# Hybrid decoder block on one core: row statistics spread by DMA, the merge moved into the next step, squares in two fp32r parts

## The reference, cut to what matters

```python
q = rmsnorm(qkv[:, :, 0], q_norm_g[i]) * scale
k = rmsnorm(qkv[:, :, 1], k_norm_g[i])
...
for g, (window, dilation) in enumerate(ATTN_PATTERNS):
    o_g, lse_g = dilated_window_attention(q[:, :, g], k[:, :, g], v[:, :, g], slopes[g], window, dilation)
...
# inside: m = max(s); p = exp(s - m); den = sum(p); o = p @ v / den; lse = m + log(den)
wgt = jax.nn.softmax(jnp.stack(lses, axis=0), axis=0)
o_attn = jnp.sum(wgt[..., None] * jnp.stack(outs, axis=0), axis=0)
```

## Time and profile before

| what | us |
|---|---|
| median of 3 runs | 1835.39 |
| lowest and highest | 1834.36, 1835.42 |
| the profiled execution, whole | 1834.99 |
| its span in the profile | 1833.2 |
| TensorE busy in the span | 1788.0 (98%) |
| VectorE, ScalarE, GpSimd busy | 1024.3, 561.8, 828.6 |

### The profile page before, as it was taken

How to read it: one execution, slowest core, us unless ns; L and a number is a source line. 1 busy time by engine, 2 the same in 40 slices (tenths; PEclk the granted TensorE clock), 3 DMA queues, 4 the chain that set the end, 5 groups by cost and what they waited for, 6 DMA issues and landing times.

```text
span 1833.2 us, 23679 instructions
## 1 busy us (share of the span) xinstructions
PE 1788.0 (98%) x8628; PEld 1420.7 (77%) x8628; DVE 1024.3 (56%) x1545; ACT 561.8 (31%) x1069; POOL 828.6 (45%) x597
## 2 busy tenths in 40 slices
PE   8999999999999987999999999999999999999997
PEld 6777777777777766788888888788888888888786
DVE  6346645564655488343313323787787887644644
ACT  6533444354245423111411222533333333000000
POOL 7536443644544374554225734265455455222221
PEclk9999999999999999999999999999999999999999
DMA  4111111211121023445412244322232232345211
GB/s 173 36 41 47 52 53 41 64 52 41 41 58 47 24 70 93 112 114 132 144 64 70 92 141 169 138 82 90 69 93 79 69 103 92 137 150 194 81 54 49
DMA packets 64192, 158.08 MB, mean 86 GB/s; under 512 B 10912, under 2 KB 27680, under 8 KB 64112
## 3 DMA queue, kind: packets, MB, share of 16 engines
q1 hardware_dynamic: 51856, 145.35, 24.5%
q10 hardware_dynamic: 11792, 10.04, 1.9%
q0 software_dynamic: 464, 1.62, 0.2%
HBM read 123.54 MB, written 32.26 MB: 85 GB/s over the span
## 4 chain that ended last, share of the span: by engine, by line
PE 85%; DVE 8%; issue 3%; POOL 2%; DMA 1%; ACT 1%; SPq 0%; DVEq 0%; POOLq 0%
PE bank L911 13%; PE bank L912 13%; PE bank L913 13%; PE bank L1276 7%; PE bank L1278 7%; PE bank L1277 7%; PE bank L1334 4%; PE bank L1336 4%; PE bank L1335 4%; PE bank L925 2%; PE bank L1059 2%; PE bank L1072 2%; PE bank L1045 2%; DVE run_z L1774 1%; PE bank L1238 1%
## 5 line engine op out<-in xcount | busy, mean ns | idle before, releaser
L911 PE MATMUL bank<-hhi,whi 128*128 128x512 f32 x1024 | 421.0, 411 | 5.6 <-DVE hlo L1711 5.6
L912 PE MATMUL bank<-hlo,whi 128*128 128x512 f32 x1024 | 404.9, 395 | 0.0
L913 PE MATMUL bank<-hhi,wlo 128*128 128x512 f32 x1024 | 404.8, 395 | 0.0
L626 POOL TENSOR_TENSOR wlo<-raw,whi 128x1024 fp32r<-128x1024 f32 (+1 forms) x84 | 196.7, 2342 | 300.1 <-DVE whi L1667 298.1
L911 PEld LDWEIGHTS bank<-hhi,whi 128*128 128x128 f32 x1024 | 193.7, 189 | 52.5 <-issue 10.1
L913 PEld LDWEIGHTS bank<-hhi,wlo 128*128 128x128 f32 x1024 | 193.6, 189 | 45.4
L912 PEld LDWEIGHTS bank<-hlo,whi 128*128 128x128 f32 x1024 | 194.1, 190 | 39.5 <-issue 1.2
L1824 DVE CUSTOM_DVE_ANT_0 sp<-bank,mask 128x128 f32<-128x128 f32 (+1 forms) x192 | 56.3, 348 | 114.6 <-PE bank L1045 112.7
L1449 ACT ACTIVATE sp<-sp,negm 128x128 f32<-128x128 f32 (+1 forms) x192 | 83.9, 439 | 106.6 <-DVE negm L1828 106.5
L884 POOL TENSOR_TENSOR plo<-st,phi 128x512 fp32r<-128x512 f32 x60 | 79.5, 1328 | 58.6 <-ACT phi L1579 57.4
L2114 DVE CAST fhi<-ff 128x1024 fp32r (+1 forms) x44 | 31.4, 715 | 125.4 <-PE bank L1336 125.4
(11 more groups left out here) (304 smaller groups left out, 3927.8 us busy)
## 6 DMA issues: line engine op xcount, KB each, us to landing
raw<-in_wblocks SPq DMA_DIRECT2D x98, 512.0 KB, 3.6
pair<-in_wblocks SPq DMA_DIRECT2D x40, 512.0 KB, 4.8
ff_scr<-ffo SPq DMA_DIRECT2D x22, 512.0 KB, 5.9
ff<-ff_scr SPq DMA_DIRECT2D x22, 512.0 KB, 4.2
rt<-rt_scr SPq DMA_DIRECT2D x8, 516.0 KB, 6.6
x<-in_xT SPq DMA_DIRECT2D x8, 512.0 KB, 9.2
zb_scr<-zb SPq DMA_DIRECT2D x8, 512.0 KB, 3.3
zb<-zb_scr SPq DMA_DIRECT2D x8, 512.0 KB, 3.5
```

The lines of the kernel that those rows point to most:

```text
L626: pool.tensor_tensor(wlo[par][:, 0:cols], raw[par][:, 0:cols], whi[par][:, 0:cols].bitcast(F32), ALU.subtract).then_inc(lo_done, 1)
L911: nc.tensor.matmul(ps, a, x, start=start and k == k_list[0], stop=False)
L912: nc.tensor.matmul(ps, a, y, start=False, stop=False)
L913: last = nc.tensor.matmul(ps, b, x, start=False, stop=stop and k == k_list[-1])
```

## The change

- `sum_squares` becomes two fp32r matmuls: ScalarE writes the square twice, rounded (`sqh`) and in fp32 (`sq`); VectorE subtracts (`square_lo`, tile `sql`), between `merge_max` and the merge weights, or between `merge_psum` and `merge_z`. It moves to the end of sub-steps 2, 4, 6, 8.
- In steps 0 to 10 the copies and 16 transposes of the statistics are replaced: one transpose of both statistics (32 rows) at j = 9, a copy to SBUF by ScalarE at j = 10, and `spread` on SP: a store to DRAM, a wait for it, and four loads that write a row into 64 partitions each, into the tile `bmd` (after pattern 0 straight into `run_n` and `run_z`).
- The merge of steps 0 to 10 moves as a whole into the next step: `merge_max` and weights at j = 1 and 5, `merge_psum` and `merge_z` at j = 3 and 7, GpSimd's part at j = 4 and 8, ScalarE's exponential at j = 3 and 7. It reads `bmd` in SBUF in place of PSUM. The product with v at j = 4 and 8 waits for it. Step 11 keeps its own merge at its end and gets that of step 10 before it.

```diff
-        stat = [hx[:], rtmp[:].rearrange("p a g k -> p (a g k)")]
+        negm, den = sd[:, 0], sd[:, 1]
+        stat = [bmd[:, h, :] for h in range(2)]
+        LAST = 3 * HP - 1
...
+            def spread(a, hp, ag):
...
+                sp_.wait_ge(st_copied, a + 1)
+                sp_.wait_ge(d_read, 2 * a + 1)
+                if ag == 0 and hp:
+                    sp_.wait_ge(o_ready, 2 * hp)
...
+                sp_.dma_start(stat_scr.rearrange("i x (s q) -> (i x s) q", q=P), st_t[0:32, :]).then_inc(st_out, 16)
+                sp_.wait_ge(st_out, 16 * (a + 1))
+                for i, done in enumerate((sm_in, sz_in)):
+                    to = (run_n, run_z)[i][:, :] if ag == 0 else bmd[:, i, :]
+                    for x in range(2):
+                        sp_.dma_start(to[DH * x:DH * (x + 1)], stat_scr[i, x].unsqueeze(0).broadcast_to([DH, T])).then_inc(done, 16)
...
             for hp in range(HP - 1):
...
+                for b in range(3):
+                    loop_load(hp, b)
+                if hp:
+                    spread(3 * hp - 1, hp - 1, 2)
+                for b in range(3, 6):
+                    loop_load(hp, b)
+                spread(3 * hp, hp, 0)
+                for b in range(6, 9):
+                    loop_load(hp, b)
+                spread(3 * hp + 1, hp, 1)
+                loop_load(hp, 9)
...
+            spread(LAST - 3, HP - 2, 2)
...
+            spread(LAST - 2, HP - 1, 0)
...
+            spread(LAST - 1, HP - 1, 1)
...
             def rescale(ag, hp, h):
...
+                if ag == 2:
+                    pool.wait_ge(merged, hpc(hp, 2) + 2)
...
-                    if a and ag == 0 and j == 0:
-                        weigh(a - 1, 2, hp - 1, 1)
-                    if a and ag == 0 and j == 5:
-                        normalise(2, hp - 1, 1)
+                    if a and ag != 1 and j in (4, 8):
+                        pg, ph, h = (ag + 2) % 3, hp - (ag == 0), j // 4 - 1
+                        rescale(pg, ph, h)
+                        weigh(a - 1, pg, ph, h)
+                    if a and ag == 0 and j in (7, 10):
+                        normalise(2, hp - 1, j == 10)
+                    if a and ag == 0 and j == 10:
...
-                    if a is not None and ag > 0 and j in (10, 11):
...
+                    if n is None and j in (10, 11):
...
-                        if ag == 1 or n is None or h == 0:
-                            weigh(a, ag, hp, h)
-                        if ag == 2 and n is None:
-                            normalise(ag, hp, h)
-                        elif ag == 2 and h:
-                            normalise(ag, hp, 0)
+                        weigh(a, ag, hp, h)
+                        normalise(ag, hp, h)
...
             def sum_squares(n, gi):
...
-                pe.wait_ge(sq_done, 4 * n + gi + 1)
-                nc.tensor.matmul(b_nb[:], blk_ones, sq[:, gi % 2, :], start=True, stop=True).then_inc(ss_done, 1)
+                pe.wait_ge(sql_done, 4 * n + gi + 1)
+                nc.tensor.matmul(b_nb[:], ones_r[:], sqh[:], start=True, stop=False)
+                nc.tensor.matmul(b_nb[:], ones_r[:], sql[:], start=False, stop=True).then_inc(ss_done, 1)
...
-                    if n is not None and j in (2, 4, 6, 8):
-                        gi = (j - 2) // 2
-                        if gi == 0:
-                            pe.wait_ge(vev_done, 2 * a + 2)
-                        else:
-                            pe.wait_ge(ln_done, 4 * n + gi)
-                        sum_squares(n, gi)
-                    if a is not None and j in (9, 11):
+                    if n is None and j in (9, 11):
...
-                    if a is not None and j in (10, 11):
+                    if n is None and j in (10, 11):
...
+                                if a and s_ % 4 == 0:
+                                    pe.wait_ge(d_read, 2 * a + s_ // 4)
...
+                        if n is not None and j == 9:
+                            pe.wait_ge(ln_done, 4 * n + 4)
+                            nc.tensor.transpose(b_nb[0:32, 0:P], sd[:].rearrange("p i x s -> p (i x s)"), ident).then_inc(mt_done, 1)
+                    if n is not None and j in (2, 4, 6, 8):
+                        gi = (j - 2) // 2
+                        if gi == 0:
+                            pe.wait_ge(vev_done, 2 * a + 2)
+                        else:
+                            pe.wait_ge(ln_done, 4 * n + gi)
+                        sum_squares(n, gi)
...
             def square(n, g, b, gi):
...
-                if gi >= 2:
-                    act.wait_ge(ss_done, 4 * n + gi - 1)
-                act.activation(sq[:, gi % 2, :].rearrange("p (i r) -> p i r", r=DIL[g]),
-                               by_residue((qn if gi < 2 else kn)[g][:, :], g, gi % 2), ACT.Square).then_inc(sq_done, 1)
+                if gi:
+                    act.wait_ge(ss_done, 4 * n + gi)
+                x = by_residue((qn if gi < 2 else kn)[g][:, :], g, gi % 2)
+                act.activation(sqh[:].rearrange("p (i r) -> p i r", r=DIL[g]), x, ACT.Square)
+                act.activation(sq[:, gi % 2, :].rearrange("p (i r) -> p i r", r=DIL[g]), x, ACT.Square).then_inc(sq_done, 1)
...
+            def weights_exp(ag, hp, h):
...
+                act.wait_ge(ab_in, 4 * hp + 2 * (ag - 1) + h + 1)
+                act.activation(ab[h][:], ab[h][:], ACT.Exp).then_inc(ab_exp, 1)
...
             def slot(n, g, b, a, ag, hp):
                 for j in range(12):
+                    if a and ag != 1 and j in (3, 7):
+                        weights_exp((ag + 2) % 3, hp - (ag == 0), j // 4)
...
-                    if a is not None and ag and j >= 10:
-                        h = j - 10
-                        act.wait_ge(ab_in, 4 * hp + 2 * (ag - 1) + h + 1)
-                        act.activation(ab[h][:], ab[h][:], ACT.Exp).then_inc(ab_exp, 1)
-                        if ag == NPAT - 1 and h:
+                    if a is not None and n is not None and j == 10:
+                        act.wait_ge(mt_done, a + 1)
...
+                        act.activation(st_t[0:32, :], b_nb[0:32, 0:P], ACT.Copy).then_inc(st_copied, 1)
+                    if a and ag == 0 and j in (5, 9):
+                        reciprocal_z(hp - 1, NPAT - 1, j == 9)
+                    if n is None and j >= 10:
+                        weights_exp(ag, hp, j - 10)
+                        if j == 11:
...
-                    if a and ag == 0 and j == 3:
-                        reciprocal_z(hp - 1, NPAT - 1, 1)
...
+                if first:
+                    act.wait_ge(merged, 4 * HP + 2)
...
             def ublock(hp, n):
-                a = 3 * hp + 1
-                merge_psum(a, 1, hp, 1)
-                evict_u(hp, n, 0)
-                merge_z(a, 1, hp, 1)
-                evict_u(hp, n, 1)
+                for h in range(2):
+                    evict_u(hp, n, h)
...
             def merge_max(a, ag, hp, h):
-                dve.wait_ge(mt_done, 2 * a + h + 1)
-                nn, ps = natural(run_n[:, :], ag, h), split2(b_nb[:], ag)
                 if ag == 0:
-                    V.tensor_copy(nn, ps).then_inc(m_read, 1)
...
+                if a == LAST:
+                    dve.wait_ge(mt_done, LAST + h + 1)
+                else:
+                    dve.wait_ge(sm_in, 32 * (a + 1))
+                nn, new = natural(run_n[:, :], ag, h), split2(b_nb[:] if a == LAST else half(bmd[:, 0, :], h), ag)
+                up = split2(ab[h][:, 1, :], ag)
...
-                link(TT(up, nn, ps, ALU.subtract))
-                TT(nn, nn, ps, ALU.min).then_inc(m_read, 1)
+                link(TT(up, nn, new, ALU.subtract))
+                link(TT(nn, nn, new, ALU.min))
+                if a == LAST:
+                    dve.sem_inc(m_read, 1)
...
+            def merge_weights(a, ag, hp, h):
+                if ag == 0:
+                    return
+                down, up = (split2(ab[h][:, i, :], ag) for i in range(2))
...
             def merge_psum(a, ag, hp, h):
...
-                dve.wait_ge(dt_done, 2 * a + h + 1)
+                if a == LAST:
+                    dve.wait_ge(dt_done, h + 1)
+                else:
+                    dve.wait_ge(sz_in, 32 * (a + 1))
...
-                    V.tensor_copy(nm, split2(b_o[h][:], ag))
-                    V.tensor_copy(nz, split2(b_t[:], ag)).then_inc(d_read, 1)
+                    V.tensor_copy(natural(num[:, :], ag, h), split2(b_o[h][:], ag)).then_inc(d_read, 1)
...
-                TT(t_z[:], b_t[:], ab[h][:, 1, :], ALU.mult).then_inc(d_read, 1)
+                TT(t_z[:], b_t[:] if a == LAST else half(bmd[:, 1, :], h), ab[h][:, 1, :], ALU.mult).then_inc(d_read, 1)
...
             def merge_z(a, ag, hp, h):
...
+            def square_lo(n, gi):
...
+                dve.wait_ge(sq_done, 4 * n + gi + 1)
+                if n or gi:
+                    dve.wait_ge(ss_done, 4 * n + gi)
```

(65 more changed lines are left out.)

39 lines of the change are left out of this document (20 added, 19 removed).

## The result

| | before | after |
|---|---|---|
| median, us | 1835.41 | 1868.12 |
| lowest and highest | 1834.36, 1840.44 | 1866.6, 1875.66 |
| ratio, 95% interval | | 1.0182 [1.0167, 1.0198] |
| start of step 11 in the trace | 644.6 | 654.8 |

The change makes the kernel 32.7 us slower: about 1.6 ahead of step 0, 8.6 in steps 0 to 10, 22.6 from step 11 on (1213.4 for 1190.8, median less start of step 11). In what follows "busy" is TensorE's busy time in the trace, "idle" the rest, and "clock" is busy time x (1 - granted clock), summed over stretches of 2 us, that is the time lost because TensorE ran at the lower of its two clock levels.

A forecast was written before the change was run, and what follows sets the result against it. TensorE was taken to bound the kernel between 60 and 640 us, without idle time. From 1834.99, less 40.2, plus 48.5 of stalls and 20 in the last step, came 1863.3, say 1864; range 1834 to 1886.

The forecast's parts named there:

- Removed from TensorE: Cheaper sums (21.1 us) and fewer transposes (18.1) in steps 0 to 10, about 1.0 ahead of step 0; together 40.2.
- Stalls in steps 0 to 10: TensorE waits added by the subtraction and merge chains: 53.8 us less 5.3 existing, 48.5 more; bounds 19.2 and 70.
- The first sum's 2.9: TensorE's wait for VectorE's first subtraction in merging steps with pattern 0 or 2 running, behind `min`: 2.9 us.
- the third with pattern 2 running: In steps 2, 5, 8, turns ahead of the third sum make TensorE wait 3.2 us.
- pattern 1's 1.3: In steps 1, 4, 7, 10 the first subtraction waits for GpSimd's split, without `merge_max` ahead: 1.3 us.
- The stalls put down to ScalarE in steps 3, 6 and 9: TensorE waits for ScalarE's chain at sub-steps 4, 6 and 8: 0.8, 1.2 and 1.5 us per step.
- The last step: Step 11 runs step 10's moved merge in turns with GpSimd; copies end at +55.4 us, cost +20, bound +28.
- turns: VectorE operations with two SBUF inputs and GpSimd operations each wait for the other's whole instruction; `min` then takes 3.1 us.
- DMA path: Statistics stored and broadcast by DMA arrive before they are needed: cost 0, bounds 0 and 5 us per merging step.
- 1 wanted no turns: Rival: GpSimd's operations fall where VectorE has none from SBUF, added stalls stay under 36 us; 1812 us, chance 14%.
- 2 wanted half of the turns: Rival: half of the counted cost in the last step and in sub-steps 4 to 8; 1840 us, chance 16%.
- 4 said the sums are no cheaper: Rival: two fp32r matmuls cost as much as the fp32 one, 21 us of saving gone; 1885 us, chance 3%.

The follow-up runs named there:

- merge10_own: The changed kernel, with step 10 keeping its own statistic copies, sixteen transposes and merge as before the change; 1848.6 us, ratio 1.0066 to the kernel before.
- tables_late: The changed kernel, with GpSimd's three tables of step 11 moved to the end of j = 8; 1863.2 us, ratio 1.0145 to the kernel before.
- broadcast_twice: The changed kernel, with the four statistic broadcasts issued twice and readers waiting for the second set; 1866.9 us, ratio 1.0167 to the kernel before.
- split_held: The changed kernel, with GpSimd's split of a step's second weight block held until VectorE's first subtraction is done; 1858.6 us, ratio 1.0122 to the kernel before.
- filled: The changed kernel, with nine extra fp32r matmuls ahead of sums that wait for the subtraction; 1863.0 us, ratio 1.0145 to the kernel before.
- merge10_fp32_held: The changed kernel with step 10's own statistics and merge, fp32 sums, and GpSimd's split held until the merge's first weights are issued; 1817.6 us, ratio 0.9891.
- sq_only_held: The kernel before with only the two-part squares added, and GpSimd's second split held until the first subtraction is done; 1838.2 us, ratio 1.0007.
- sq_only: The kernel before with only the two-part squares added, statistics and merge as before; 1836.4 us, ratio 1.0003.
- lo_first_merge: The changed kernel, with the subtraction ahead of `merge_max` at j = 1 and 5 alone; 1871.6 us, ratio 1.0195 to the kernel before.

## Why the prediction was right

The direction, the place and the time (1864 for 1868.1) held, and so did the mechanism. Some sizes did not, and they cancel: beside the sum of the prediction, the stalls of the steps came 19 us lower, the saving on TensorE (with the four sums ahead of step 0) 9.6 us smaller, the clock took 9.4, the last step 2.6 more, and 2.1 are not explained. That the total came out within 5 us is luck in good part. Term by term:

- **Removed from TensorE.** Transposes: 18.1 predicted, 19.0 measured (1.73 x 11). Sums: 21.1 predicted, 13.2 measured. The step that failed is "44 sums in steps 0 to 10 go from 0.95 to 2 x 0.23": the pair takes 0.55, and the twelve matmuls ahead of the scores 2.97 for 2.88.
- **Stalls in steps 0 to 10.** 48.5 predicted, 29.5 measured by idle time between 60 and 640, plus 9.4 of clock that the prediction had no term for. So its own sign "TensorE idle 50 us or more between 60 and 640" did not come: it was 34.8. The first sum's 2.9 came as 2.5 to 2.6; the third with pattern 2 running, 3.2 predicted, as 2.5 and 1.9; pattern 1's 1.3 as 0.9 to 1.4. The stalls put down to ScalarE in steps 3, 6 and 9 (0.8, 1.2 and 1.5) were far too large: 10.5 us for the three steps, where `ptr` ended 3.6. The third sum there, 1.5 predicted, waited 0.7.
- **By step.** Step 0 changed by -2.6 (predicted -2.3), pattern 1's steps by -1.2 to -1.6 (-1.6), pattern 2's by +4.7 (+3.4), pattern 0's later ones by +0.6 to +1.2 (+2.6). The four sums ahead of step 0 did not gain 1.0, they lost 1.6, with two waits of 1.5. By parts, -32.2 of work, +29.3 of idle time and +9.4 of clock make +6.5 in steps 0 to 10, and 8.6 was measured; 2.1 stay unexplained.
- **The last step.** +20 predicted, +22.6 measured; copies ended +52.0 into it, not +55.4. About 5 of it are clock, for which the prediction had no term here either. `merge10_own` shows the cause (19.6 of it). That turns are a part of it is shown by `tables_late` (the copies begin 11.9 us earlier in the step, 4.9 are left at the end); how much is turns and how much is only more work on VectorE's path was not separated.
- **DMA path.** 0, shown by `broadcast_twice`.
- **Rivals.** 1 wanted no turns: `min` at 3.03 and the 22.6 of the last step rule it out, though its bound for the steps (added stalls under 36) was met. 2 wanted half of the turns in the later sub-steps and in the last step: for the steps it was the better number (35 for the 29.5 measured, where the forecast had 48.5), for the last step the worse (10 for 22.6). 4 said the sums are no cheaper; they are, by 0.3 each, so a third of its 21 us was true.
- **The mechanism.** `split_held` shows the turns directly: the same operation with the same inputs, 3.03 with the split running, 1.07 without. Two SBUF inputs are not needed: the weights, with a single one, took 0.43 alone and 1.91 to 2.52 beside GpSimd, and four copies took 8.80. The Trainium skill ("GPSIMD Engine Reference", § 1 Specifications) also names VectorE instructions "in a 2-port perf mode"; these times fit that, but no run here shows in which mode an instruction ran.

## What to carry to other kernels

When TensorE has no idle time, put a new wait into the sum with two prices: its length, and the matmuls behind it at half rate. The second is paid only in part where TensorE would have had to wait soon after anyway (`filled`: 5.8 back of 9.4). Before adding a short VectorE operation to a critical chain, look at what GpSimd starts just then; a whole GpSimd instruction may stand ahead of it, and holding that instruction back can be worth more than the change itself (14.2 us for 5.1 in `merge10_fp32_held`). It can also only move the collision to another operation and gain nothing (`sq_only_held`), so look at what the held instruction meets next. Before moving work out of a step where it hides, check the last step of the loop, which has nothing to hide it.

## What the runs showed of the hardware

- A short wait of TensorE may or may not cost clock. In the changed kernel, of eight between 2.48 and 2.64 us five were followed by 1.5 to 3.0 us lost at the 1.2 GHz level, three by none. In `sq_only` two of the three waits of 1.75 were followed by 1.7 lost; in `lo_first_merge` the three of 2.96 to 3.02 by nothing and the three of 2.82 by 1.7 each. In `split_held`, in steps 3 and 6, waits of 1.33 and 0.54 close together were followed by 1.5 to 1.6. Steps 0 to 10 of `tables_late`, the same program there, lost 14.0 us in its trace and not 9.4.
- Nine useless matmuls ahead of each of nine sums saved 5.8 us in all.
- An fp32 sum costs 0.95, two fp32r ones 0.55 and not 0.46, as the first starts 0.32 ahead of the second.
